# The rotation of the differential heads: a partition shuffle on VectorE in place of a permutation product on TensorE

## The reference, cut to what matters

```python
def apply_partial_rope(x, cos, sin):
    r = cos.shape[-1]
    x1, x2, rest = x[..., :r], x[..., r:2 * r], x[..., 2 * r:]
    return jnp.concatenate([x1 * c - x2 * s, x2 * c + x1 * s, rest], axis=-1)

q = apply_partial_rope(rms_norm(q.reshape(b, t, 2 * DIFF_HEADS, DIFF_QK), q_head_g), cos, sin)
k = apply_partial_rope(rms_norm(k.reshape(b, t, 2 * DIFF_HEADS, DIFF_QK), k_head_g), cos, sin)
```

## Time and profile before

| | |
|---|---|
| runs | 2266.0, 2273.48, 2285.97 us |
| profiled execution | span 2264.6 us from first to last instruction; the page gives no other time of it. It is 1.4 us under the shortest run and 8.9 us under the median |
| TensorE matmuls | busy 2067.8 us, 91% of the span |
| VectorE, ScalarE, POOL | busy 48%, 36%, 44% |
| granted TensorE clock, mean | 0.976 of full speed |

### The profile page before, as it was taken

One profiled execution on the slowest core, in us unless ns is written; L12 is line 12 of the kernel. 1 busy time (PEld: TensorE's weight loads), 2 busy tenths in 40 slices (PEclk: granted clock), 3 DMA queues, 4 the chain that ended last, 5 costly groups with the idle time before them and its releaser, 6 DMA issues.

```text
span 2264.6 us, 32615 instructions
## 1 busy us (share of the span) xinstructions
PE 2067.8 (91%) x13298; PEld 1785.2 (79%) x13298; DVE 1076.7 (48%) x1653; ACT 820.2 (36%) x1344; POOL 996.6 (44%) x592
## 2 busy tenths in 40 slices
PE   7999998888778999999989999987878789999999
PEld 7888887567657999999988888874556567888887
DVE  8632355565565644442038332554665656444400
ACT  3322343576564322222223322443674633222221
POOL 4355432784312344444434454335861334444444
PEclk9999999999899999999999999999998999999999
DMA  4211111000001222323322111111001012223333
GB/s 156 71 57 57 57 48 66 10 1 19 21 18 38 93 85 93 94 85 95 101 75 84 56 57 56 47 38 56 1 1 38 19 56 93 93 93 96 100 103 112
DMA packets 40036, 143.79 MB, mean 63 GB/s; under 512 B 4433, under 2 KB 4561, under 8 KB 39761
## 3 DMA queue, kind: packets, MB, share of 16 engines
q1 hardware_dynamic: 39888, 141.72, 19.6%
HBM read 139.60 MB, written 2.10 MB: 63 GB/s over the span
## 4 chain that ended last, share of the span: by engine, by line
PE 71%; DVE 13%; ACT 7%; issue 6%; POOL 2%; DMA 1%; ACTq 0%; SPq 0%; DVEq 0%; POOLq 0%
PE pb L844 43%; PE pb L879 6%; PE pb L880 6%; PE pb L881 6%; DVE kh L1868 2%; ACT ebuf L1460 2%; PE pb L1279 2%; DVE rowmax L1920 1%; DVE proj L1850 1%; PE pb L1287 1%; POOL parts L626 1%; ACT rstd L1428 1%; PE pb L1219 1%; PE pb L979 1%; ACT ebuf L1471 1%
## 5 line engine op out<-in xcount | busy, mean ns | idle before, releaser
L626 POOL TENSOR_TENSOR parts<-raw,parts 128x1024 fp32r<-128x1024 f32 x248 | 604.7, 2439 | 831.6 <-ACT parts L1516 831.4
L844 PE MATMUL pb<-mix,parts 128*128 128x264 f32 x4608 | 675.1, 296 | 44.2 <-POOL parts L626 17.5
L844 PEld LDWEIGHTS pb<-mix,parts 128*128 128x128 f32 x4608 | 613.2, 195 | 71.5 <-issue 28.6
L1516 ACT ACTIVATE parts<-raw 128x1024 fp32r<-128x1024 f32 x248 | 262.3, 1058 | 822.7 <-PE pb L844 521.2
L844 PE MATMUL pb<-proj_r,parts 128*128 128x264 f32 x3104 | 429.5, 286 | 0.5 <-POOL parts L626 0.5
L844 PEld LDWEIGHTS pb<-proj_r,parts 128*128 128x128 f32 x3104 | 401.7, 190 | 0.8 <-issue 0.7
L879 PE MATMUL pb<-proj_r,parts 128*128 128x512 f32 x528 | 207.7, 393 | 0.8 <-DVE mbuf L1850 0.8
L881 PE MATMUL pb<-proj_r,parts 128*128 128x512 f32 x528 | 207.9, 394 | 0.0
L880 PE MATMUL pb<-proj_r,parts 128*128 128x512 f32 x496 | 197.9, 399 | 0.0
L1856 DVE TENSOR_TENSOR h<-h,pb 128x528 f32<-128x528 f32 (+1 forms) x48 | 33.3, 693 | 273.2 <-PE pb L844 142.2
L1850 DVE TENSOR_TENSOR mbuf<-pb,rstd 128x528 f32<-128x528 f32 (+1 forms) x44 | 30.8, 700 | 215.1 <-PE pb L844 110.8
(11 more groups left out here) (276 smaller groups left out, 2849.6 us busy)
## 6 DMA issues: line engine op xcount, KB each, us to landing
raw<-w_stream SPq DMA_DIRECT2D x250, 512.0 KB, 3.5
w_head<-w_heads SPq DMA_DIRECT2D x8, 512.0 KB, 4.8
h<-x_t SPq DMA_DIRECT2D x8, 264.0 KB, 6.7
out_t<-h SPq DMA_DIRECT2D x8, 256.0 KB, 4.7
con<-consts SPq DMA_DIRECT2D x1, 1652.5 KB, 10.1
par<-params SPq DMA_DIRECT2D x1, 340.0 KB, 4.2
con<-consts SPq DMA_DIRECT2D x1, 128.0 KB, 6.7
```

The costliest lines, as they stand in the source:

```text
L626: nc.gpsimd.tensor_tensor(parts[:, n % PARTS, 1, :], w, parts[:, n % PARTS, 0, :].bitcast(FP32), ALU.subtract).then_inc(split.sem, 1)
L844: last = nc.tensor.matmul(pb[rows_, 2 * p + a, 0:HALF], lhs_t, rhs[:, a * HALF:(a + 1) * HALF], start=start, stop=stop)
L1516: nc.scalar.activation(parts[:, n % PARTS, 0, :], raw[:, r % RAW, :], ACT.Copy).then_inc(lead_ready.sem, 1)
```

## The change

TensorE's permutation product goes, and with it the signals `rot_ready` and `rot_used`. VectorE, at the end of a differential tile's norm, waits for its own multiplication and shuffles the tile into BM: within each block of 32 partitions it swaps 0 to 7 with 8 to 15 and leaves the others. In the rotation it multiplies BM in place by the sines, and adds as before. The sign that `perm_d` carried is put into `sin_d` once, by two instructions in layer 0 (`sine_signs`). POOL's cosines wait for the shuffle instead of the product.

```diff
+SWAP = [*range(DIFF_ROPE // 2, DIFF_ROPE), *range(DIFF_ROPE // 2), *range(DIFF_ROPE, 32)]
@@ POOL
             def cosines(l, j):
                 t = NORMS[j][1]
-                pool.wait_ge(rs_used.sem, rs_used.at(l, j + 1))
-                pool.wait_ge(rot_ready.sem, rot_ready.at(l, t + 1))
+                pool.wait_ge(swapped.sem, swapped.at(l, t + 1))
@@ TensorE
             def norm(l, j):
-                if j and NORMS[j - 1][0] == "d":
-                    pe.wait_ge(rot_used.sem, rot_used.at(l, NORMS[j - 1][1] + 1))
-            def turned(l, j):
-
-                pe.wait_ge(log_ready.sem, log_ready.at(l, RS_N + j + 1))
-                pe.wait_ge(rs_used.sem, rs_used.at(l, j + 1))
-                product(2, C("perm_d"), tile_of(proj, DQ + NORMS[j][1]), True, True).then_inc(rot_ready.sem, 1)
...
-                pe.wait_ge(rot_used.sem, rot_used.at(l, 8))
@@ VectorE
+            def sine_signs():
+
+                link(nc.vector.reduce_sum(rowmax[:, 0:1], C("perm_d"), axis=AX.X))
+                nc.vector.tensor_scalar(C("sin_d"), C("sin_d"), rowmax[:, 0:1], -1.0, ALU.mult, ALU.mult).then_inc(signed.sem, 1)
...
             def norm(l, j):
...
+                if what == "d":
+                    dve.wait_ge(rs_used.sem, rs_used.at(l, j + 1))
+                    dve.wait_ge(roped.sem, roped.at(l, t))
+                    nc.vector.stream_shuffle(tile_of(proj, BM), tile_of(proj, tile), SWAP).then_inc(swapped.sem, 1)
 
             def turned(l, j):
 
                 t = NORMS[j][1]
                 sines = tile_of(proj, BM)
-                dve.wait_ge(rot_ready.sem, rot_ready.at(l, t + 1))
-                nc.vector.tensor_tensor(halves(sines), pair(2), halves(C("sin_d")), ALU.mult).then_inc(rot_used.sem, 1)
-                dve.wait_ge(rot_used.sem, rot_used.at(l, t + 1))
+                dve.wait_ge(swapped.sem, swapped.at(l, t + 1))
+                dve.wait_ge(signed.sem, 1)
+                link(nc.vector.tensor_tensor(sines, sines, C("sin_d"), ALU.mult))
                 dve.wait_ge(qcos.sem, qcos.at(l, t + 1))
                 nc.vector.tensor_tensor(tile_of(proj, DQ + t), tile_of(proj, DQ + t), sines, ALU.add).then_inc(roped.sem, 1)
@@ VectorE, layer 0, after the tile MISC
                         if l == 0:
                             row_factors()
                             column_table()
+                            sine_signs()
```

More of the change, by code:

```diff
@@ L534, in trunk @@
         o_ready = signal("o_ready", NT)
-        rot_ready = signal("rot_ready", 8)
-        rot_used = signal("rot_used", 8)
+        swapped = signal("swapped", 8)
+        signed = signal("signed", 0)
         roped = signal("roped", 8 + 2 * MLA_H)
@@ L1163, in ml_job @@
                     norm(l, n)
-                elif what == "turned":
-                    turned(l, n)
             for l in range(DEPTH):
```

## The result

The kernel after took 2280.95 us in the median of 20 runs (2272.45 to 2288.7), the kernel before 2274.97 us in 20 runs beside them (2262.67 to 2285.97). The ratio is 1.0034, interval 1.0021 to 1.0048: 7.7 us longer (of 2274.97; the two medians are 6.0 us apart), between 4.8 and 10.9, no change by the bound of 1%. The profiled execution after has a span of 2279.8 us, 15.2 more than that of before; by the ratio, about half of this belongs to the two executions that were profiled.

A forecast was written before the change was run, and what follows sets the result against it. VectorE's queue, not TensorE, was taken to set the time in the rotations. Layer 0 +1.6, layer 1 +3.3 and clock +1.7 gave +6.6 us on the median 2273.5, so 2280 us; range about 2263 to 2292.

The forecast's parts named there:

- The shuffle's price: On VectorE, each of 16 added shuffles of 128x528 float32 takes 0.75 us, with the wait for the multiplication before it.
- dearer shuffle: Rival: a shuffle takes up to 1.70 us ahead of 14 stores, 13.3 us more, 2293 us; chance 0.10.
- Stores behind norms: The shuffle stands before the next tile's store, so groups start late: slot 64 +0.64, slot 68 +1.1, slot 76 +1.9 us.
- Slots 60 to 84: Delays at slots 64 to 76 pass to slot 78's norm, and tile 5's multiplication ends late: +1.6 us a layer.
- Slot 88, local: TensorE finishes slot 86 early, but VectorE's and POOL's queue delays slot 88's store: +0.6 us layer 0, +2.3 layer 1.
- Behind slot 88: Slots 88 to 97: delay shrinks 0.4 at 92, shuffles cost 0.5, slot 97's product gives 0.70; together -0.6 us a layer.
- The clock: TensorE's idle time of some 4 us ahead of slot 88 is followed by a lower clock: +1.7 us, taken once.
- gain of slot 97: Slot 97's removed product, inside a group with nothing waiting, gives TensorE 0.70 us.
- layer 1's first half: Layer 1 up to the end of tile 5's multiplication: the delay passed to slot 78 was put at +1.6 us.
- `sine_signs`: Two short instructions behind the store at 73 us, hidden by VectorE's 3.67 us of idle time: nothing.
- Slight gain: Rival: POOL and VectorE get past each other, slot 88 comes 1 to 2 us early, 2271 us; chance 0.27.
- Nothing visible: Rival: a shuffle of 0.43 us fits most gaps the product leaves, +2 us, 2276 us; chance 0.08.

The follow-up runs named there:

- hold_split_88: Kernel after, with POOL's split of slot 88 waiting for the addition of slot 86, once a layer: 2269.24 us, ratio 0.9995 to the kernel before.
- openings_only: Kernel after, with POOL's cosines and the addition ahead of the split at slots 64, 68, 72, 76, 92, slot 88's split not held: 2269.83 us, ratio 0.9995.
- late_hold_88: Kernel after, with the shuffle moved behind the tile's store and POOL's split of slot 88 held until tile 5's addition: 2273.99 us, ratio 1.0012.
- product_kept: Kernel after, with TensorE's permutation product put back as dead work, POOL's cosines waiting for it, its result unread: 2271.88 us, ratio 1.0014.
- before_cos_first: Kernel before, with POOL's cosines and the addition ahead of the split at openings with a rotation, slot 88's split held too: 2262.80 us, ratio 0.9971.

## Why the prediction was right, and where it was right by luck

The predicted change of 6.6 us stands against 7.7 [4.8 to 10.9]; the sum for the stretches, 1.6 + 3.3 us without the clock, against 1.5 + 3.2 with it. Since the clock took its part, terms have compensated. Point by point:

- **The shuffle's price** (0.75) was right: 0.746. By the Trainium skill (VectorE: DVE Perf Modes, the perf-mode tier table) I had an estimated 0.6 to 0.7; the row is a little above it. The dearer shuffle is refuted, and a running split does not hold it (0.76).
- **Stores behind norms.** Slot 64 +0.64 forecast, +0.7 measured; slot 68 +1.1 and +1.2; slot 76 +1.9, but only +1.1 / +0.7: POOL's delay passed on less than I let it.
- **Slots 60 to 84** (+1.6 a layer, to the end of tile 5's multiplication): +1.7 and -1.4. The term was too high, and layer 0 came out by luck. The norm of slot 78 starts only 0.7 and 0.4 us later than before (46.9 and 47.3 us into the stretch before, 47.6 after), where +1.6 was to arrive. The rest is the clock's place. Before, 3.4 us of the lower level fall behind that norm's wait in both layers, and its 24 matmuls take 4.80 and 4.58 us. After, layer 0 has 6.8 us there (5.23 us). In layer 1 the 3.4 us fall on the matmuls of slots 76 and 77, ahead of the wait, which shrinks from 2.22 us (layer 0) to 0.71, and the 24 matmuls run at the full clock. Before and after, TensorE in layer 1:

```profile
1481.58 4.58 PE L844 MATMUL pb<-mix,parts 128*128 128x264 f32 x24
...
1492.96 3.30 PE L844 MATMUL pb<-mix,parts 128*128 128x264 f32 x24
```

  hold_split_88, which is the kernel after up to here, has no low clock in layer 0 up to slot 84, and its store of slot 84 is where layer 1's is (60.1 us).
- **Slot 88, local.** From the end of tile 5's multiplication to the group of slot 88 it took 6.6 and 5.0 us before, 7.0 and 7.0 after: +0.3 and +2.0, where +0.6 and +2.3 were forecast. The mechanism was right too (the split pulled forward, VectorE's two-input instructions and POOL's in line, some 4 us of waiting: 4.05). The order within was not: I had the split ahead of the sines, and in both layers the sines and the cosines came first and the split then passed the addition. hold_split_88 shows that mending this place is worth as much as the whole loss (openings_only shows the same of the openings). In layer 1 the 2.0 us come ahead of any low clock of that place, so the low clock alone is not the cause; it adds the 4.2 us behind.
- **Behind slot 88** (-0.6 a layer): -0.5 and +2.6. Two terms are in it, both mis-sized. The product of slot 97 was put at 0.70 us; the last stretch between stores shrank from 9.0 to 6.9 us, by 2.1 in both layers. I had counted TensorE and forgotten VectorE's queue. The kernel before, layer 0, VectorE:

```profile
376.52 0.71 DVE L2163 TENSOR_TENSOR proj<-pb,con 128x528 f32<-128x528 f32 x1 [2.71 <-PE pb L844]
...
378.70 3.45 DVE L1904 TENSOR_REDUCE hs<-ebuf 128x4 f32<-128x512 f32 x5
382.07 0.70 DVE L1850 TENSOR_TENSOR proj<-pb,rstd 128x528 f32<-128x528 f32 x1
```

  The sines waited for a product in the middle of the group, behind them came 3.45 us of reductions, and only then the last store, 1.2 us after TensorE had finished (376.13 + 4.75 = 380.88). After, the reductions end before TensorE does, and the store waits for it:

```profile
382.29 3.44 DVE L1893 TENSOR_REDUCE hs<-ebuf 128x4 f32<-128x512 f32 x5
386.50 0.71 DVE L1839 TENSOR_TENSOR proj<-pb,rstd 128x528 f32<-128x528 f32 x1 [0.77 <-PE pb L844]
```

- **The clock** (+1.7, once): from the store of slot 88 to that of slot 92 the four stretches take 10.0 and 10.0 us before, 11.6 and 14.2 after. That is +1.6 and +4.2, in both layers and not once, with 3.4 and 10.2 us at the lower level behind the wait. This term was sized too low by some 4 us, and the gain of slot 97 (2.8 too low for both) and layer 1's first half (3 us below the forecast) made up for it. That the sum came out is luck in that much.
- **`sine_signs`** at nothing was right, but the order was not: the two instructions lie at 72.81 and 73.13 us, ahead of the store and not behind it, which so comes at 73.89 instead of 72.83; 1.63 us of idle time follow. late_hold_88, which has them, reaches layer 0's stretch at 279.04 us with 6.8 us of low clock on the way, the kernel before at 279.07 with as much.
- **The rivals.** Slight gain: the way in which it could come, POOL and VectorE getting past each other, is real, but needs an edit, and hold_split_88 with a ratio of 0.9995 only comes back to the kernel before. Nothing visible: the ratio's interval excludes 1. The range's upper end should have been 2293 (2280 + 13.3), not 2292.

Left open: 3 us of the 7.7 that the stretches of one profile do not hold, and why the delay of the stores shrank to 0.7 and 0.4 us by slot 78.

## What to carry to other kernels

Before taking work off the busiest engine, look at what releases it next. Here TensorE's products filled gaps ahead of VectorE's store, held a buffer back just long enough for POOL's split to come behind the addition, and kept the clock up at slot 88; with the queues mended their removal was worth 3.3 us in the one stretch in which the clock did not fall, and nothing in the whole time (0.9962 and 0.9963 without, 0.9971 with them). An operand moved from PSUM to SBUF turned a multiplication that took 0.71 us beside POOL's split into one of 2.80. And where a wait is removed, ask which queue entry now goes first. The 0.3 to 0.4% that was to be had lay in the order of POOL's jobs, in both kernels alike.

## What the runs showed of the hardware

- **Who goes first.** With a VectorE instruction waiting for the cosines and the split next in POOL's own queue, the split won in all eight such places of the kernels (355.64 against 355.79 here), and the addition took 2.76 us. POOL can be held too: the cosines, 1.30 us alone, took 2.55 beside the addition of squares and the sines.
- **Small instructions are held to the split's end.** A scaling of 16x4 elements (`den`), 0.15 us where no POOL instruction runs, took 0.95 to 1.90 us beside a split, in the kernel before too (1.79), and ended with it: at 373.09 us in the kernel after, the split at 373.07. The row of late_hold_88, VectorE in slot 92, issued 0.51 us behind the split's start:

```profile
362.12 1.89 DVE L2133 SCALAR_TENSOR_TENSOR den<-kh 16x4 f32<-16x4 f32 x1
```

- **The clock after a wait at slot 88.** In the eight stretches in which TensorE waited 4.0 to 4.5 us there, the lower level came each time, for 3.4 to 10.2 us; in six of them it began within the wait. In the ten with waits of 1.4 to 2.8 us it followed in six. In the six of before, product_kept and before_cos_first, which begin the group without a wait, it did not come between the group's start and the next store. From the store of slot 88 to that of slot 92 the kernel after lost 1.6 us with 3.4 us at the lower level, and 4.2 with 10.2.
